# A two-layer block stack on one core: the side work of a chunked recurrence in other places of its rounds, and its inputs with three value tiles at once

## The reference, cut to what matters

```python
def step(state, inp):
    r_t, w_t, k_t, v_t, a_t, b_t = inp
    sa = jnp.einsum('bhvk,bhk->bhv', state, a_t)
    state = state * w_t[:, :, None, :] + sa[..., None] * b_t[:, :, None, :] + v_t[..., None] * k_t[:, :, None, :]
    y = jnp.einsum('bhvk,bhk->bhv', state, r_t)
    return state, y
```

## Time and profile before

| | |
|---|---|
| median of 3 runs | 2808.7 us (2799.99 to 2811.71) |
| profiled execution, its own time | 2806.8 us |
| its span in the profile | 2804.9 us |
| TensorE clock granted, mean | 0.995 of full |
| PE busy | 2689.7 us, 96% |
| DVE, ACT, POOL busy | 50%, 45%, 44% |
| the stretch with the recurrence's inputs, 580 to 770 us | PE busy 170.6 of 190 us |
| the 32 rounds, 770 to 1224 us | PE busy 410.9 of 454 us |

### The profile page before, as it was taken

The page is one execution under the profiler, slowest core; times in us unless marked ns, Lnnn a source line. Parts: engine busy times, 40 slices in busy tenths (PEclk is TensorE's granted clock), DMA queues, the critical chain, the costliest instruction groups (busy, mean ns, idle before and its releaser), DMA issues.

```text
span 2804.9 us, 55468 instructions
## 1 busy us (share of the span) xinstructions
PE 2689.7 (96%) x23340; PEld 2150.6 (77%) x23340; DVE 1408.2 (50%) x2497; ACT 1263.3 (45%) x2284; POOL 1244.1 (44%) x1148
## 2 busy tenths in 40 slices
PE   8999999989989999989999999899999999999999
PEld 6677888857777777777888877587777777788887
DVE  6847885055667777754888112702223333244410
ACT  5754443234566666544444225634444453422221
POOL 5234444545743434315444445054443644544443
PEclk9999999999999999999999999999999999999999
DMA  5112322322200000103323322032222322333322
GB/s 176 42 53 90 98 91 90 98 90 90 88 16 6 7 8 7 35 23 91 98 92 93 94 90 78 9 114 74 75 76 68 98 83 85 96 98 91 96 89 78
DMA packets 67079, 208.64 MB, mean 74 GB/s; under 512 B 14736, under 2 KB 15376, under 8 KB 66448
## 3 DMA queue, kind: packets, MB, share of 16 engines
q1 hardware_dynamic: 63680, 192.96, 22.4%
q0 software_dynamic: 2576, 10.78, 1.1%
q10 hardware_dynamic: 576, 1.35, 0.1%
HBM read 199.69 MB, written 4.19 MB: 73 GB/s over the span
## 4 chain that ended last, share of the span: by engine, by line
PE 86%; DVE 7%; ACT 3%; POOL 2%; issue 2%; DMA 0%; SPq 0%; DVEq 0%; ACTq 0%; POOLq 0%
PE banks L1765 22%; PE banks L1767 22%; PE banks L1766 22%; PE banks L807 6%; PE banks L816 1%; PE banks L1916 1%; POOL low L321 1%; ACT arena L1163 1%; PE banks L1978 1%; PE banks L873 1%; PE banks L1964 1%; DVE low L550 1%; PE banks L1953 1%; DVE arena L2779 1%; PE banks L1802 1%
## 5 line engine op out<-in xcount | busy, mean ns | idle before, releaser
L321 POOL TENSOR_TENSOR low<-arena,high 128x256 fp32r<-128x256 f32 (+3 forms) x820 | 968.5, 1205 | 1155.9 <-ACT high L309 1155.8
L1765 PE MATMUL banks<-high,high 128*128 128x512 f32 (+1 forms) x2736 | 1083.4, 396 | 9.7 <-DVE arena L2643 2.9
L1767 PE MATMUL banks<-high,low 128*128 128x512 f32 (+1 forms) x2736 | 1073.0, 392 | 0.0
L1766 PE MATMUL banks<-low,high 128*128 128x512 f32 (+1 forms) x2736 | 1072.8, 392 | 0.0
L309 ACT ACTIVATE high<-arena 128x1024 fp32r<-128x1024 f32 (+1 forms) x376 | 382.0, 1016 | 798.0 <-PE banks L1767 796.4
L1765 PEld LDWEIGHTS banks<-high,high 128*128 128x128 f32 x2736 | 514.6, 188 | 138.4 <-DVE arena L2643 5.0
L1767 PEld LDWEIGHTS banks<-high,low 128*128 128x128 f32 x2736 | 514.5, 188 | 119.8
L1766 PEld LDWEIGHTS banks<-low,high 128*128 128x128 f32 x2736 | 514.8, 188 | 118.1 <-issue 1.9
L2677 DVE TENSOR_TENSOR arena<-banks,arena 128x512 f32<-128x512 f32 x48 | 33.1, 692 | 424.5 <-PE banks L1767 423.4
L807 PE MATMUL banks<-arena 64*64 64x64 f32 x5632 | 207.0, 222 | 38.5 <-ACT arena L1163 31.5
L2808 DVE SCALAR_TENSOR_TENSOR arena<-arena 128x511 f32<-128x511 f32 x88 | 237.1, 2694 | 3.1
(11 more groups left out here) (313 smaller groups left out, 3076.8 us busy)
## 6 DMA issues: line engine op xcount, KB each, us to landing
arena<-weights SPq DMA_DIRECT2D x301, 512.0 KB, 3.5
arena<-weights SPq DMA_DIRECT2D x48, 448.0 KB, 3.2
arena<-weights SPq DMA_DIRECT2D x28, 256.0 KB, 2.6
arena<-tables POOLq DMA_DIRECT2D x5, 448.0 KB, 3.6
arena<-x_t SPq DMA_DIRECT2D x4, 512.0 KB, 5.8
x_spill<-arena POOLq DMA_DIRECT2D x1, 2048.0 KB, 9.3
arena<-x_spill POOLq DMA_DIRECT2D x1, 2048.0 KB, 8.9
out_t<-arena SPq DMA_DIRECT2D x8, 256.0 KB, 4.1
```

What stands on the lines that cost most here:

```text
L321: low = pool.tensor_tensor(lo[:, part], ring[w % RING][:, part], hi[:, part].bitcast(F32), ALU.subtract)
L1765: pe.matmul(dst, hi[:, c], x[0], start=kt == 0, stop=False)
L1766: pe.matmul(dst, hi[:, c], x[1], start=False, stop=False)
L1767: mm = pe.matmul(dst, lo[:, c], x[0], start=False, stop=kt == kts_of[t] - 1)
```

## The change

Five parts.

1. **PE's side work has other places.** `side(i, place)` takes the place of `aux`, `aux_gate` and `aux_left`. By round c: c=0: ss at the masks (as before), the bonus ahead of the first merge, `lora` sw0 between the first merge and the growth, sa0 between the second merge and the growth. c=1: two matmuls of sw1 ahead of the first merge, the third behind it, sa1 behind the second merge. c=2: two matmuls of the gate at the masks, two ahead of the first merge. c=3: the turns, as before. The waits for `PP[1]` stand ahead of its next use.
2. **The state's sums** of both directions go to one bank, `PP[0]`. The second direction's matmuls stand behind those of the first and behind half the output, and PE waits for the first (`S0`) ahead of them.
3. **DVE and ACT follow:** the scan of decays is cut into two halves (U3, U4), `exclusive` goes from U6 to U5, the a-factors go one slot on, `y_var` goes to the next round, `rkk` and the copy of the bonus to c=0. On ACT sigmoids, exponentials, `rstd` and the gate's weights change places.
4. **Inputs:** the first three value tiles go together (`three_tiles`, the third two feature tiles behind, in bank 3 of its own), and for the last two value tiles the split of weights three tiles on (those are the first two tiles of k) is made ahead of the eviction.
5. In the third block one feature tile of a filler goes from step 16 of a loop to ahead of it (`fill("c", 3, 5)`).

```diff
+        def side(i, place):
+            j, c = i // TT, i % TT
+            bank, more = PP[1], j + 1 < KT
+            at_ = (c, place)
+            if at_ == (0, "masks") and more:
+                if j >= 2:
+                    od.wait(pe, j - 2, "y")
                 ss(j + 1, bank)
+            elif at_ == (0, "last sum") and more:
+                rd.wait(pe, j + 1, "mx")
                 bonus(j, bank)
...
+            elif at_ == (0, "merge 1") and more:
                 bd.wait(pe, j, "bon")
+                lora(j + 1, "sw0", bank)
+            elif at_ == (0, "merge 2") and more:
+                ra.wait(pe, j + 1, "sw0")
+                lora(j + 1, "sa0", bank)
+            elif at_ == (1, "last sum") and more:
+                ra.wait(pe, j + 1, "sa0")
+                lora(j + 1, "sw1", bank, 0)
+            elif at_ == (1, "merge 1") and more:
+                lora(j + 1, "sw1", bank, 1)
+            elif at_ == (1, "merge 2") and more:
+                ra.wait(pe, j + 1, "sw1")
+                lora(j + 1, "sa1", bank)
+            elif at_ == (2, "masks") and j >= 2:
...
+                gate(j - 2, bank, 0)
+            elif at_ == (2, "last sum") and j >= 2:
+                gate(j - 2, bank, 1)
...
@@ advance_state
-            for k in (() if last else (1, 0)):
-                for h in range(2):
-                    for d in range(2):
-                        g = d ^ q
-                        mm = pe.matmul(PP[d][hf(h), P:P + C], R.TK[it % 2][hf(g), d, P * k + C * h:P * k + C * h + C],
+            def state_sum(d):
+                g = d ^ q
+                for k in (1, 0):
+                    for h in range(2):
+                        mm = pe.matmul(PP[0][hf(h), P + C * d:P + C * d + C], R.TK[it % 2][hf(g), d, P * k + C * h:P * k + C * h + C],
                                        values(it, c, q, g, h) if k else R.SA[hf(g), h, :], start=k == 1, stop=k == 0)
+                return mm
             if not last:
-                pc.inc(mm, "S")
+                pc.inc(state_sum(0), "S0")
             for h in range(2):
+                if h and not last:
+                    pc.wait(pe, st, "S0")
+                    pc.inc(state_sum(1), "S")
                 for p in range(2):
@@ the rounds on PE
-                aux(i, 1)
+                side(i, "last sum")
                 merge(i, 1)
+                side(i, "merge 1")
                 for h in range(2):
                     grow(i, h, 5)
-                aux_gate(i)
             if seq:
                 solve(i - 1, 1)
             if off:
                 merge(i, 2)
+                side(i, "merge 2")
                 for h in range(2):
                     grow(i, h, 6)
-                aux_left(i, 1)
@@ ACT, per round
+                if c == 2 and more:
+                    factor(j + 1, "er0")
+                if c == 3 and more:
+                    factor(j + 1, "F")
...
+            if off and c in (0, 1) and more:
+                sigmoid(j + 1, f"sa{c}", PP[1])
@@ DVE, spread
             elif at_ == (1, "U3") and more:
-                decay_sums(j + 1, 0)
+                decay_sums(j + 1, 0, slice(0, T // 2))
             elif at_ == (1, "U4") and more:
+                decay_sums(j + 1, 0, slice(T // 2, T))
                 chunk_sums(j + 1, 0)
             elif at_ == (1, "U5") and more:
                 centre(j + 1, 0)
-            elif at_ == (1, "U6") and more:
                 exclusive(j + 1, 0)
...
             elif at_ == (2, "U5"):
+                if j >= 2:
+                    z_gate(j - 2, PP[1])
                 if more:
                     centre(j + 1, 1)
-                if j >= 2:
-                    z_gate(j - 2, PP[1])
-            elif at_ == (2, "U6") and more:
-                exclusive(j + 1, 1)
+                    exclusive(j + 1, 1)
+            elif at_ == (3, "M") and prev:
+                y_var(j - 1)
@@ the inputs
+        def three_tiles(t, rhs, gate, behind):
+            lead = [(t, 0), (t + 1, 0), (t + 2, behind)]
+            for u, _ in lead:
+                wait_bank(pe, u)
+                pe.wait_ge(w_low, pieces_of[u][0] + 1)
+            for n in range(KT + behind):
+                if n < KT:
+                    gate(n)
+                for u, late in lead:
+                    kt = n - late
+                    if not 0 <= kt < KT:
+                        continue
...
@@ copy_tiles on ACT; split_first is (6, 7) for the values
                 wait_tile(act, t)
+                if k in split_first:
+                    advance(t)
@@ third block
-                fill("c", 3, 4)
+                fill("c", 3, 5)
```

More of the change, by code:

```diff
@@ L704, in ss, with lora @@
             rp.inc(pe.matmul(bank, blk, rn, start=True, stop=True), "ss")
-        def lora(j, n, bank):
+        def lora(j, n, bank, part=None):
             d = int(n[2])
@@ L751, in aux @@
                 bonus(j, bank)
[L752 to L758, removed]
-                bd.wait(pe, j, "bon")
[L760 to L770, removed]
+            elif at_ == (0, "last sum"):
+                od.wait(pe, j - 2, "y")
+                bonus(j, bank)
+            elif at_ == (0, "merge 1") and more:
+                bd.wait(pe, j, "bon")
+                lora(j + 1, "sw0", bank)
[11 more added lines that the diff above has]
+            elif at_ == (2, "masks") and j >= 2:
+                if more:
+                    ra.wait(pe, j + 1, "sa1")
+                else:
+                    bd.wait(pe, j, "bon")
+                gate(j - 2, bank, 0)
+            elif at_ == (2, "last sum") and j >= 2:
+                gate(j - 2, bank, 1)
+            elif at_ == (3, "masks") and j:
@@ L771, in aux_left @@
                 if j >= 2:
                     td.wait(pe, j - 2, "z")
-            elif slot == 6 and j:
+                else:
+                    ra.wait(pe, j + 1, "sa1")
+                turn_y(j - 1, "bt", bank)
+            elif at_ == (3, "last sum") and j:
                 oa.wait(pe, j - 1, "zt")
-            elif slot == 7 and j:
-                od.wait(pe, j - 1, "y")
+                turn_y(j - 1, "yt", bank)
         def scores(i):
@@ L966, in pe_rwkv @@
             if off:
-                aux(i, 0)
+                side(i, "masks")
                 square(i, 0, 1)
@@ L1115, in copy @@
         def copy(name, k):
-            copy_tiles(name, dsts[name], funcs.get(name, ACT.Copy), only=k, buffers=1)
+            copy_tiles(name, dsts[name], funcs.get(name, ACT.Copy), only=k, buffers=1,
+                       split_first=(KT - 2, KT - 1) if name == "rw_v" else ())
         for i, (name, _) in enumerate(VARIANTS):
@@ L1203, in act_rwkv @@
                     norm_k(j + 1)
-                if c == 3 and more:
-                    factor(j + 1, "ea1")
+                if c == 3 and j:
+                    shifted_bonus(j - 1, PP[1])
             if seq:
@@ L2142, in hn_tiles, with copy_tiles @@
                 act.activation(r, r, ACT.Exp, bias=ZB, scale=-0.5).then_inc(HN_RS, 1)
-        def copy_tiles(name, dst, func=ACT.Copy, only=None, buffers=2, ahead=True):
+        def copy_tiles(name, dst, func=ACT.Copy, only=None, buffers=2, ahead=True, split_first=()):
             for k, t in enumerate(tiles_of[name]):
@@ L2158, in copy_tiles @@
                 act.activation(d, src, func).then_inc(copied, 1)
-                if ahead:
+                if ahead and k not in split_first:
                     advance(t)
```

140 lines of the change are left out of this document (71 added, 69 removed).

## The result

| | before | after |
|---|---|---|
| median of 20 runs each, us | 2808.1 | 2812.35 (2807.07 to 2817.43) |
| ratio after to before | | 1.002, 95% interval 1.0014 to 1.0026 |
| profiled execution, its own time, us | 2806.8 | 2807.07 |
| its span, us | 2804.9 | 2805.2 |

The change makes the kernel slower by 4.2 us in the medians; by the interval of the ratio it is 3.9 to 7.3 us. I had forecast 2806.7, no change. The result lies outside the forecast's own range (2803 to 2810) and inside the bounds (2796.5 to 2815.5); the sign is clear, and it is not the one of my sum (-0.1). The profiled execution of the changed kernel is the fastest of its 20, so its total tells nothing; its stretches do.

The account below looks back on a forecast made before the run. The prediction took PE (TensorE), busy 96% of the span, to bound the kernel. Recurrence +1.6 and inputs -1.7 gave -0.1 us on 2806.8, so 2806.7; own range 2803 to 2810, bounds 2796.5 to 2815.5.

Parts of the forecast that it names:

- my sum (-0.1): Whole kernel: +1.6 us for the recurrence and -1.7 for the inputs, together -0.1 on 2806.8.
- The new wait, s: In advance_state: one-bank sums with PE waiting for its own result cost 0.23 us more each, between 0.10 and 0.35.
- The term for the inputs: Ahead of the recurrence: values -1.1, keys -0.3 and filler -0.3, in all -1.7 us.
- The bound from above: Upper limit of the new cost of an advance_state, 0.35 us: the release as long as the 0.15 tile change on top.
- the sum by rounds: Recurrence, each j from 2 to 6: c=0 +1.21, c=1 -0.17, c=2 -1.19, c=3 +0.03, together -0.12 us.
- The rivals: Four alternatives: self-wait nearly free (2800, chance 0.2), costs more (2813, 0.15), VectorE the bound (2814, 0.1), inputs gain in full (2804, 0.15).
- My terms without s: Rounds c=0 to 3: what PE gains or loses by the side work's new places, apart from the sums' new cost.
- the sum for the recurrence: All rounds: -0.6 for j=2 to 6, +1.4 for j=0 and 1, +0.56 for j=7, +0.23 last half round: +1.6 us.
- -1.4 for values and keys: Inputs: -1.1 us from an earlier fourth value tile, -0.3 net for keys, between -2.4 and +0.3.
- What would show it: List of signs in the profile after, such as waits for ACT, round lengths and gaps, that would prove the forecast right or wrong.
- The self-wait costs more: Rival in advance_state: the new cost is 0.35 us, 6.2 us more in all, 2813; chance 0.15.
- VectorE becomes the bound: Rival in the rounds: side work between two U's no longer fits, +7 us, 2814; chance 0.1.

Follow-up runs that it names:

- experiment 1: Kernel before with only the one-bank state sum (both directions in PP[0], PE waiting for the first): 2830.8 us against 2807.9, ratio 1.0083.
- experiment 2: Kernel before with only the order of the state sum changed, one direction after the other, both banks kept, no wait: 2814.0 us, ratio 1.0024.
- experiment 4: Kernel before with only the changed inputs and the filler (parts 4 and 5): 2807.0 us, ratio 0.9999.
- experiment 5: Changed kernel without parts 4 and 5, so only the recurrence is changed: 2811.7 us, ratio 1.0015 to the kernel before.
- experiment 6: Changed kernel with the second direction's sum and its wait behind other work, the first interleaved with output: 2804.5 us, ratio 0.9988 to the kernel before.
- experiment 3: Changed kernel with each direction's sum interleaved with output matmuls of the other 64 rows, wait kept: 2807.7 us, ratio 0.9999 to the kernel before.
- experiment 9: Kernel before with the early split of weights and the filler, without three value tiles: one single run of 2806.5 us.
- experiment 7: Experiment 6 with the q=1 second sum back right behind the output, only the q=0 wait hidden: 2805.0 us, ratio 0.9991 to the kernel before.
- experiment 10: Experiment 6 with two value tiles side by side instead of three, early split kept: 2802.2 us, ratio 0.9983 to the kernel before.

## Why the prediction was wrong, by its own steps

The step that failed is **"The new wait, s"**, in size and in count, and a second error of the other sign, in what the new places gain, hid half of it. The term for the inputs failed too.

- *Size.* I took 0.23, with 0.35 as the upper bound. It is 0.43 (experiment 1), 0.15 of it the order (experiment 2) and 0.28 the wait. The rate of 0.026 us per matmul that I used for eight of one direction is that of `L921` in the earlier trace rows, where matmuls of both row halves alternate. The bound from above left this out too, though the text spoke of a "worse interleave".
- *Count.* I wrote 32 + 24 = 56 sums, seven for a j, but the sum by rounds has only five (2, 1, 1, 1), and none for j=7, 36 in all. It also had the round with one sum wrong: that is c=0, not c=1. At my own 0.23 the missing 20 would have made the forecast 4.6 us longer, 2811.3, within 1.1 us of the result, which would have been luck: the price and the gains were off as well. The rivals counted 52 of them. With 56 x 0.43 = 24 for my 36 x 0.23 = 8.3, the term was 16 us short.
- *Places.* The difference of the changed kernel to experiment 1, which has the same sums, is what the places, DVE's and ACT's order give in each round: +0.60, -0.70, -1.67, -0.47, in all -2.24 for a j. My terms without s were +0.75, -0.40, -1.42, -0.20: -1.27. The signs and the order hold, each round is 0.15 to 0.3 better than I counted. I kept c=1 and c=3 small because of D and of DVE; since the sums come late in both kernels, D is later in experiment 1 and there is more for the side work at the masks to cover. No run isolates that reason, but the traces bear on it. In rounds c=3 D starts 2.66 us behind the first matmul of the step before it in the kernel before, 3.14 in experiment 1 and 2.54 in the changed kernel, and PE's squares after 2.99, 3.48 and 2.99: with `exclusive` away from DT the later sum costs nothing there. In j=7 I expected +0.56; the rounds c=0 to c=2 took 46.44 in experiment 1, some 1.4 of it at half clock (1213.9 to 1217.3), and 44.93 after, nearly the same. From round 0 to round 31 the difference is 477.48 - 459.67 = 17.8 us, some 2.8 of it that stretch and one in j=0 of experiment 1: 15.0, where I had about 7 for the whole recurrence.
- *Together:* about 16 us too little for the wait, about 8 too little for the gain, so by these terms the sum for the recurrence was some 8 us too low; the rounds 0 to 31 say about 6 (7.0 for my 1.4 without the last half round), and the difference of the medians was 4.3 above my -0.1. That the forecast was near in time though its largest term was off by three times is luck: two errors of opposite sign.
- *Inputs.* -1.4 for values and keys is not what the change gave: counted from POOL's split of the fourth value tile it is 0 in this profile. I had -1.1 for the values and they cost 1.07: the fourth tile starts 4.60 us behind that split and not 5.14, 0.5 us less, and the half rate behind its gap, for which I had put nothing there, takes about 1.5. For the keys I had -0.3 and they gave 1.06. The filler's 0.7 us less idle (0.92 for the 1.61 of the earlier trace rows) came, though I had -0.3 for it. The medians show none of it clearly: -0.9 us with both bounds around nothing (experiment 4), +0.7 in the changed kernel (2812.35 for the 2811.66 of experiment 5).
- *What would show it:* waits for ACT at 15 to 20 us (17.6), c=0 longer by 1 (1.01), a hole in the output (0.18), slow matmuls behind a gap at 664: right. c=2 shorter by 1: 0.78. The fourth value tile at 614.6: 613.8, in an execution that was 1.3 us early.
- *Rivals.* "The self-wait costs more", with a chance of 0.15, is what happened, but that the time agrees, 2812 for its 2813, is luck: its price, 0.35, its count and the gains beside it are not the measured ones. "VectorE becomes the bound" falls for the change as made: PE waits 3.1 us for D where it waited 4.0, and 1.5 for the U's (L834) where it waited 1.6. D is part of what limits experiment 6.
- The way from the last matmul of the first sum to the first behind the wait is 0.29 us (848.70 to 848.99), where I had 0.22 + 0.06 for the matmul and its release. That part of s was well sized; what was short is the rate of the matmuls around it. The Trainium skill, "TensorEngine Tiling (Array Packing)" under Gotcha 1, says that different row tiles cannot use one PSUM bank at the same time and leaves the order to software. That names why the wait stands there, though no run here leaves it out; what it costs is the 0.28 us above.

## What to carry to other kernels

Where small matmuls run on quarters of the array, price a new dependence by the spacing of starts with and without it, and price the order too: matmuls that no longer alternate between row halves cost half as much again as the wait did. A table of waits can improve by 15 us while the kernel gets slower, because a wait of PE for its own result, shorter than a matmul's modelled end, isn't in it. Count how often a term occurs in the same table in which it is summed, and check the total against the count: here that alone would have turned the sign. Before a wait is hidden behind other work, look what is left of it in the stream, here half, and when the next engine's chain, counted from the same first matmul, will be done. And count a gain from an event ahead of the change: two executions can lie 1.3 us apart before anything changed runs.

## What the runs showed of the hardware

- PE waiting for its own result between two groups of 64x64 matmuls that write one bank from different row halves: 0.28 us for each wait (experiments 1 and 2, the single bank with it), with a hole of 0.18 us in the starts at q=0, and 0.31 where the output stood in the first sum and not behind it (experiment 3).
- Eight 64x64 matmuls on one row half, then eight on the other, rather than alternating: 0.15 us more for each group of 16 with its output (experiment 2). The first matmuls of a direction start over 0.29 us, and 14 alternating ones of the kernel before over 0.18 us (0.40 - 0.22).
- Idle gaps of PE of 3.9 to 4.0 us were followed, in all eleven cases in the twelve profiles, by 3.4 us or twice that in which the 512-column matmuls started every 0.43 us rather than every 0.235, the engine at 1.2 GHz: at once (656.02 in the earlier trace rows) or 1.3 us behind the gap (613.81, slow from 615.1). Gaps of 3.3 us were followed by it in four profiles (666.80 in the changed kernel; experiments 3, 6 and 9) and not in three (experiments 4, 7 and 10). A stretch of 3.4 us cost 1.3 to 1.5 us where two kernels or rounds differ by it alone (experiment 10; the round c=2 of j=5 before, 16.89 for 15.58). What fills an idle time only in part can so give its gain back.
- One kernel's executions differ by up to 12 us, and two profiled ones by half-rate stretches of 3.4 and 10.2 us at places where nothing in the code differs enough to account for it. Groups of 11 or more runs had mean granted clocks from 0.9936 to 0.9962. What sets these was not tested.
